# Differential attention in the second block of a two-block transformer kernel: scores kept in PSUM under a 64x64 corner mask, one square root for all heads, the first branch product placed ahead of the second branch's turns

## The reference, cut to what matters

```python
def differential_attention(q, k, v, lam, lam_init, subln_g):     # 4 heads, 512 tokens, blocks of 128 rows
    key_chunk = jnp.arange(s) // 64
    def block(args):
        qa, qb, bi = args
        q_chunk = (bi * 128 + jnp.arange(128)) // 64
        mask = key_chunk[None, :] <= q_chunk[:, None]
        s1 = (qa @ k1) * scale;  s2 = (qb @ k2) * scale
        p1 = softmax(where(mask, s1, -1e30));  p2 = softmax(where(mask, s2, -1e30))
        return (p1 - lam * p2) @ v
    out = rms_norm(out, subln_g) * (1.0 - lam_init)               # over each head's 128 columns
...
g_a, g_b = split(sigmoid(g + b_gate))
merged = g_a * (o_a @ w_branch_a) + g_b * (o_b @ w_branch_b)      # o_a: chunked attention with a relative bias
x = layer_norm(ALPHA * x + merged @ w_out)
```

## Time and profile before

| what | value |
|---|---|
| median of 3 runs | 2563.78 us (2562.53 to 2566.39) |
| the profiled execution's own time | 2561.58 us |
| its span, first to last instruction | 2559.7 us |
| mean granted TensorE clock | 0.95 |
| PE busy | 2356.5 us, 92% of the span |
| DVE / ACT busy | 1691.4 / 1241.1 us |
| attention B, first mask addition to last probabilities | 1906.3 to 2002.7 us |
| from there to the first branch product | 2002.7 to 2017.2 us |
| first branch product | 2017.2 to 2040.9 us |

### The profile page before, as it was taken

The page is one execution under the profiler, slowest core; times in us unless marked ns, Lnnn a source line. Parts: engine busy times, 40 slices in busy tenths (PEclk is TensorE's granted clock), DMA queues, the critical chain, the costliest instruction groups (busy, mean ns, idle before and its releaser), DMA issues.

```text
span 2559.7 us, 29221 instructions
## 1 busy us (share of the span) xinstructions
PE 2356.5 (92%) x10384; PEld 1851.3 (72%) x10384; DVE 1691.4 (66%) x1740; ACT 1241.1 (48%) x1214; POOL 414.1 (16%) x296
## 2 busy tenths in 40 slices
PE   5989876999999999999999999679998898999995
PEld 3649554788888888888888888566765676878874
DVE  4535446889988998899988998443556536333423
ACT  1123213676777677767776777332337532322320
POOL 2030043112222222212221222020200011000001
PEclk9999976999999999999999999879989898999998
DMA  7010153899999999999999999712210133122210
GB/s 283 1 50 1 57 193 118 320 387 370 371 370 386 375 370 370 384 379 368 369 385 377 370 368 361 235 70 78 80 36 34 65 121 111 66 99 99 99 66 33
DMA packets 141554, 555.04 MB, mean 217 GB/s; under 512 B 11200, under 2 KB 12352, under 8 KB 124528
## 3 DMA queue, kind: packets, MB, share of 16 engines
q1 hardware_dynamic: 129968, 512.46, 52.5%
q0 software_dynamic: 10368, 37.49, 5.8%
q10 hardware_dynamic: 1152, 4.19, 0.4%
HBM read 525.80 MB, written 28.31 MB: 216 GB/s over the span
## 4 chain that ended last, share of the span: by engine, by line
PE 87%; DVE 7%; ACT 3%; POOL 1%; issue 1%; DMA 1%; SPq 0%; POOLq 0%; ACTq 0%; DVEq 0%
PE PS L361 83%; PE PS L646 1%; PE PS L640 1%; DVE act L1489 1%; ACT act L1400 1%; DVE act L1492 1%; POOL act L2063 1%; DVE st L1477 1%; DVE small L1939 1%; DVE act L1937 1%; PE PS L516 1%; ACT L1411 0%; PE PS L818 0%; DVE ring_parts L1851 0%; DMA act<-ln_emb_b 0%
## 5 line engine op out<-in xcount | busy, mean ns | idle before, releaser
L361 PE MATMUL PS<-act_parts 128*128 128x512 f32 (+1 forms) x3300 | 1058.9, 398 | 14.2 <-issue 7.5
L1768 DVE TENSOR_TENSOR low<-ring,act_parts 128x2048 fp32r<-128x2048 f32 x396 | 886.2, 2292 | 38.3 <-ACT act_parts L1270 38.3
L361 PEld LDWEIGHTS PS<-act_parts 128*128 128x128 f32 (+1 forms) x3300 | 617.8, 189 | 177.7 <-issue 42.3
L1270 ACT ACTIVATE act_parts<-ring 128x2048 fp32r<-128x2048 f32 x396 | 731.7, 1911 | 11.1 <-PE PS L361 10.8
L361 PE MATMUL PS<-low,act_parts 128*128 128x512 f32 x1584 | 619.7, 391 | 0.0
L361 PE MATMUL PS<-act_parts,ring_parts 128*128 128x512 f32 x1216 | 380.8, 403 | 6.6 <-DVE act_parts L1991 3.7
L361 PEld LDWEIGHTS PS<-low,act_parts 128*128 128x128 f32 x1584 | 299.3, 189 | 58.3
L1851 DVE TENSOR_TENSOR ring_parts<-ring,ring_parts 128x4096 fp32r<-128x4096 f32 x30 | 132.7, 4423 | 231.8 <-ACT ring_parts L1339 231.7
L361 PEld LDWEIGHTS PS<-act_parts,ring_parts 128*128 128x128 f32 x1216 | 234.9, 193 | 70.1 <-issue 12.1
L361 PE MATMUL PS<-ring_parts,act_parts 128*128 128x512 f32 x1088 | 264.8, 397 | 12.3 <-DVE act_parts L2007 6.7
L361 PEld LDWEIGHTS PS<-ring_parts,act_parts 128*128 128x128 f32 x1088 | 207.3, 191 | 60.0 <-DVE act_parts L2007 7.1
(11 more groups left out here) (220 smaller groups left out, 1878.5 us busy)
## 6 DMA issues: line engine op xcount, KB each, us to landing
ring<-w_gate_up SPq DMA_DIRECT2D x264, 1024.0 KB, 8.0
ring<-w_down SPq DMA_DIRECT2D x132, 1024.0 KB, 7.4
ring<-w_ff SPq DMA_DIRECT2D x16, 2048.0 KB, 7.7
ring<-w_in SPq DMA_DIRECT2D x12, 2048.0 KB, 8.8
ring<-w_o SPq DMA_DIRECT2D x1, 4096.0 KB, 23.0
ring<-w_out SPq DMA_DIRECT2D x2, 2048.0 KB, 7.6
acc_d<-act SPq DMA_DIRECT2D x5, 512.0 KB, 2.6
act<-x SPq DMA_DIRECT2D x4, 512.0 KB, 4.9
```

The source lines that it names most:

```text
L361: return eng.matmul(o, lhsT, rhs, start=first, stop=last, **kw)
L1270: A_(W1hi[c % CS], W1[c], ACT.Copy).then_inc(sem["high"], 1)
L1768: tt(W1lo[c], W1[c], W1hi[c % CS].bitcast(F32), ALU.subtract).then_inc(sem["low"], 1)
```

## The change

1. Masking. `masked` waits for both score products, writes -1e30 with one memset into the 64x64 corner of both PSUM banks, and takes both maxima with one reduction over the two banks. The additions, the mask tile and POOL's two memsets are gone; POOL's signal is now `angles_done`. `scores_b` begins at an even bank, so that the two banks are neighbours. The exponentials read PSUM and write SBUF, and now the score banks come free with `expb`, not with the mask addition.
2. Normalisation. `square_b` leaves the sum of squares in one of 16 columns and copies the raw output to SBUF, which frees the bank (`ob_raw`). `out_b` is gone. After the loop ACT takes one square root of 16 columns, DVE one reciprocal, and `scale_heads` multiplies four 128x512 tiles by it. The gain `subg` is a column of one element per partition now and is applied in the high and low parts of the second half (`heads_high(1)`, `heads_low(1)`).
3. Order. Half A of the outputs is turned in iteration u = 16 of the loop, and the first branch product waits for its four low parts alone. Half B is turned after the fourth of the eight blocks of that product. On DVE the split of chunk 9 stands after the fourth of the branch multiplications, behind the low parts of half B; before, it stood ahead of all eight. On ACT the square root stands ahead of the sigmoids, and `heads_high(1)` behind them. `o2hi` and `o2lo` have a place of their own for each half.

A helper `affine` is added and not called. Core of the diff:

```diff
             def scores_b(u):
+                cur[0] += cur[0] % 2
...
-                    free[b] = past("sb_masked", 2 * u + m + 1)
+                    free[b] = past("expb", 2 * u + 2)
...
+            def turn_heads(g):
+                for t in range(NT):
+                    eng.wait_ge(*(past("ob_out", t + 1) if g else past("oa_out", UA)))
+                    b = next_bank(8 if g else 6)
+                    eng.wait_ge(*free[b])
+                    free[b] = past("o2T_lo", NT * g + t + 1)
+                    for j in range(4):
+                        ins = eng.transpose(PS[:, b, j * P:(j + 1) * P], XN[:, t, (4 * g + j) * P:(4 * g + j + 1) * P],
+                                            ident)
+                    ins.then_inc(put("o2T_psum", b), 1)
...
+                if u == UB:
+                    turn_heads(0)
...
-                eng.wait_ge(*past("o2T_lo", 2 * NT))
+                eng.wait_ge(*past("o2T_lo", NT * (br_ + 1)))
...
+                    if br_ == 0 and f == 3:
+                        turn_heads(1)
...
             def probs_b(u):
                 eng.wait_ge(*past("maxb", u + 1))
+                eng.wait_ge(*(past("pTb_psum", u - 1) if u >= 2 else past("pTa_psum", UA)))
                 for m, e in enumerate((e1b, e2b)):
-                    A_(e[:, u % 2, 0:n], e[:, u % 2, 0:n], ACT.Exp, scale=DH ** -0.5,
+                    b = bank_of("sb_psum", 2 * u + m + 1)
+                    A_(e[:, u % 2, 0:n], b[:, 0:n], ACT.Exp, scale=DH ** -0.5,
...
-                A_(hank[:, 0:P], b[:, 0:P], ACT.Square, accum_out=small[:, 24 + u % 2:25 + u % 2]).then_inc(
+                A_(hank[:, 0:P], b[:, 0:P], ACT.Square, accum_out=small[:, 48 + 4 * t + h:49 + 4 * t + h]).then_inc(
                     signal("act_step"), 1)
                 eng.wait_ge(*latest("act_step"))
-                A_(small[:, 26 + u % 2:27 + u % 2], small[:, 24 + u % 2:25 + u % 2], ACT.Sqrt,
-                          scale=1.0 / P, bias=EPS_2).then_inc(signal("ob_std"), 1)
+                A_(XN[:, t, 512 + h * P:512 + (h + 1) * P], b[:, 0:P], ACT.Copy).then_inc(signal("ob_raw"), 1)
...
+            A_(small[:, 48:64], small[:, 48:64], ACT.Sqrt, scale=1.0 / P, bias=EPS_2).then_inc(signal("ob_std"), 1)
             for f in range(KD):
                 A_(G2[:, f, :], G2[:, f, :], ACT.Sigmoid, bias=bgc[:, f:f + 1]).then_inc(signal("gate0_out"), 1)
+            heads_high(1)
             split_weights(9)
...
             def masked(u):
-                for m, e in enumerate((e1b, e2b)):
-                    tt(e[:, u % 2, 0:n], b[:, 0:n], maskb[:, S - n:S], ALU.add).then_inc(signal("sb_masked"), 1)
-                    eng.tensor_reduce(small[:, 32 + m:33 + m], e[:, u % 2, 0:n], AX.X, ALU.max).then_inc(
+                eng.wait_ge(*past("sb_psum", 2 * u + 2))
+                eng.memset(PS[0:DH, b - 1:b + 1, n - DH:n], NEG).then_inc(signal("sb_masked"), 1)
+                eng.tensor_reduce(small[:, 32:34], PS[:, b - 1:b + 1, 0:n], AX.X, ALU.max).then_inc(
...
+            scale_heads()
             for br_ in range(2):
-                split_weights((9, 11)[br_])
...
+                    if br_ == 0 and f == 3:
+                        heads_low(1)
+                        split_weights(9)
```

More of the change, by code:

```diff
@@ L1339, in split_weights, with high @@
                 A_(W2hi[n % NH], W2[n % NW], ACT.Copy).then_inc(signal("w_high"), 1)
-            def high(tag, XT):
-                for n in range(2 * NT):
+            def high(tag, XT, tiles=range(NT)):
+                for n in range(2 * tiles[0], 2 * tiles[-1] + 2):
                     t, hf = n // 2, n % 2
@@ L1419, in _ @@
                     square_b(u - 2)
+                if u == UB:
+                    heads_high(0)
                 if u < UB and u % 2:
@@ L1424, in _ @@
                         split_weights(8)
-            for n in range(2 * NT):
-                t, g = n // 2, n % 2
-                eng.wait_ge(*past("o2T_psum", n + 1))
-                A_(o2hi[:, 4 * g:4 * g + 4, o2_rows(t, g)], four(bank_of("o2T_psum", n + 1)),
-                   ACT.Copy).then_inc(signal("o2T_hi"), 1)
+            A_(small[:, 48:64], small[:, 48:64], ACT.Sqrt, scale=1.0 / P, bias=EPS_2).then_inc(signal("ob_std"), 1)
             eng.wait_ge(*past("bgc_in", 16))
@@ L1851, in split_weights, with low @@
                 tt(W2lo[n % NW], W2[n % NW], W2hi[n % NH].bitcast(F32), ALU.subtract).then_inc(signal("w_low"), 1)
-            def low(tag, XT, hi):
-                for n in range(2 * NT):
+            def low(tag, XT, hi, tiles=range(NT)):
+                for n in range(2 * tiles[0], 2 * tiles[-1] + 2):
                     t, hf = n // 2, n % 2
@@ L1983, in _ @@
                     split_weights(8)
-                if u >= 2:
-                    out_b(u - 2)
-            for n in range(2 * NT):
-                t, g = n // 2, n % 2
-                rows = o2_rows(t, g)
-                eng.wait_ge(*past("o2T_hi", n + 1))
-                tt(o2lo[:, 4 * g:4 * g + 4, rows], four(bank_of("o2T_psum", n + 1)),
-                   o2hi[:, 4 * g:4 * g + 4, rows].bitcast(F32), ALU.subtract).then_inc(signal("o2T_lo"), 1)
+                if u == UB:
+                    heads_low(0)
+            scale_heads()
             for br_ in range(2):
-                split_weights((9, 11)[br_])
                 if br_:
+                    split_weights(11)
                     split_weights(12)
```

101 lines of the change are left out of this document (56 added, 45 removed).

## The result

| | before | after |
|---|---|---|
| median of the runs, us | 2563.16 (2562.53 to 2566.39) | 2531.88 (2530.14 to 2534.67) |
| ratio, 95% interval | | 0.9879 [0.9863, 0.9894] |
| profiled execution, us | 2561.58 | 2530.14 |
| span, us; mean granted clock | 2559.7; 0.950 | 2528.3; 0.954 |

What follows compares the result with a forecast made beforehand. Attention B's chain of waits bounds the kernel, and PE its loop after the change. Loop, tail and branch 0 terms end branch 0 27.8 us earlier; 28 taken: 2561.58 to 2533.6, plus 2.2 gives 2535.8 us, range 2527 to 2545.

Steps and rivals of the forecast that it cites:

- The bound before: Attention B: a chain of mask, maximum, exponentials, mixing, copy, next mask, 23.05 us a head, with PE hardly in it.
- The loop, DVE: Attention B loop: fewer mask additions and no per-unit scaling cut the chain from 23.05 to 17.1 us a head.
- The loop, ACT: Attention B loop: 27 table loads, 34.6 us, leave ACT, few on the chain; exponentials from PSUM cost no more.
- The loop, PE: Attention B loop: PE needs 18.5 us a head against the chain's 17.1, becomes the bound; last `beside` ends at 1979.1.
- The loss to PE: Attention B loop: with PE as the bound, only 4.5 of DVE's 6 us a head count.
- The tail: Between last `beside` and branch 0: a new 2 us PE pause; branch 0 starts at 1987.2 instead of 2017.21.
- Branch 0: First branch product: 23.7 us plus 1.9 for half B's turns and 0.3 wait for chunk 9's split; ends at 2013.1.
- Contention in PSUM: Rival, loop: each exponential takes 0.3 us more, the chain grows to 19.5 a head; gain 20, time 2544; chance 0.14.
- The clock at full speed throughout: Rival, PE from the loop to branch 0: no long pause or slow beginning; gain 35, time 2529; chance 0.13.
- Order gives back part: Rival, branch 0: chunk 9's split comes late, 7 us lost before gate 1; gain 21, time 2543; chance 0.07.
- A load kept in the loop: Rival, ACT in the loop: compiler keeps a table load at each copy or square; no difference; chance 0.01.
- TensorE at 1.2 GHz throughout: Rival, loop: PE's 64.8 us take as long again, 37 us slower net, time 2600; chance 0.02.

Runs made afterwards that it cites:

- mask_and_order: Kernel after with the old normalisation put back (square root, reciprocal and scaling per unit, 27 table loads in the loop); 2545.6 us.
- after_best2: Kernel after with the splits of chunks 7 and 8 in quarters inside the loop and half A's high parts earlier; 2521.5 us, ratio 0.9836.
- norm_only: Kernel before with only the change's normalisation (one square root, scaling and gain after the loop), old masking and order; 2554.8 us.

## Why the prediction was right, and what in it was not

**The bound before** was read rightly: the chain from mask to mask. Every edit that shortened it shortened the kernel. But the way the chain takes was misread. It goes "mask, maximum, exponentials, mixing, copy, next mask" only in some units; in nine it goes through the root's table load, as here between units 12 and 13 and between 14 and 15 of the kernel before (chain of waits, start us, us, what):

```profile
1982.99 1.28 ACT L1411
...
1994.42 1.28 ACT L1411
```

**The loop, DVE.** The chain per head came out at 17.00 for 17.1, and that is luck in part. From the mask of unit 11 to that of unit 15 it takes 23.05 us before, 19.74 with the mask alone and 20.31 with the norm alone. So the masks gave 3.31 a head where 3.85 were booked, and the norm part 2.74 where 2.1 were; the two errors cancel. Successive operations of DVE overlap a little, so that from mask to scaled maxima the four units of a head shrank by 3.6 us and not 3.85; of these, with the mask alone, 0.2 are lost in unit 12, where the second table load ends behind the maxima. The prices of single operations that the sum took from the first block and from the additions held to 0.02 us.

**The loop, ACT.** "Few of them are on the chain" is the reading that failed. Of the loads, the 13 ahead of the exponentials did run beside DVE's masks, all but the one behind chunk 8's split. The other 14, ahead of the root, run beside mixing and copy, and the chain of waits passes through nine of them whole. What this was worth is another matter: mixing and copy end 0.4 us before the root at most, so the loads held DVE up for 1.6 us in five waits, 0.6 a head, and unit 8 for another 1.7 (mask_and_order against the kernel after). The prediction named these waits ("where DVE waited for the square root") and then put them at nothing. They are the greater part of the norm part's error; the 7.9 us booked for DVE's shorter queue (2.1 a head) were 7.4.

The Trainium skill, "ScalarE: Activation LUTs", section "Table sets: the hidden batching unit", says to do all exponentials together and then all square roots. That is what this part does, and the runs agree that it pays: putting 27 loads of 1.283 us and 16 roots back costs 9.4 us, for 34.6 us of loads on ACT. The 1.38 us of drain that the same page adds to a load ("What ACT_TABLE_LOAD costs") is not seen after the change either. ACT in order of time:

```profile
1985.41 1.28 ACT L1441 ACT_TABLE_LOAD   x1
1986.70 0.31 ACT L1441 ACTIVATE small<-small,colc 128x16 f32<-128x16 f32 x1
```

The root starts 0.01 us behind its load's end.

**The loop, PE.** "PE becomes the bound" was half right. PE takes 18.09 us a head (18.5 said) against the chain's 17.00. But the chain is held up at the split of chunk 8: from unit 8's mask to unit 9's it takes 1949.30 - 1939.63 = 9.67 us, 6.3 more than the 3.38 between the same two block sizes a head later. That eats its lead of 1.1 us a head, and the two arrive together: 69.9 us from first to last exponential, and PE at 1976.99. I had put 2.0 us of the split into PE's account, and a pause of 2.14 is there. The last `beside` ended at 1976.98 instead of 1979.1, and two terms are smaller than said. The slow beginning has a granted clock of 0.71 over 5.8 us, which is 1.7 of lost time and not 3.1. PE's steps were 18.09 / 4 = 4.52 a unit and not 4.63, 1.5 us over 14. With them, the measured first transposes and the measured pause the sum reads 1908.9 + 63.3 + 1.7 + 2.1 = 1976.0, 1 us short.

**The loss to PE** ("of DVE's 6 us a head only 4.5 count") did not show. The parts alone and the whole agree to 1 us. The old kernel's chain had the same split in it, and each part was cheaper or dearer than its term in the sum. A head's 6.05 us (23.05 - 17.00) are the 3.31 and 2.74 of the parts alone; what PE took back are the 0.73 us in which DVE waited for it.

**The tail.** 8.1 us from the last `beside` to branch 0 were said, 7.95 were measured, with the new wait of 2 us in its place. As a part of the change the order gained 7.8 to 8.8 us and gave 1.1 to 1.2 back.

**Branch 0.** 23.7 + 1.9 + 0.3 were said, 2011.29 - 1984.93 = 26.4 to the last gate multiplication were measured. But the four last of these run together behind chunk 9's split, so that their end says little. Gate 1's first weight load waits 0.2 us. The cover for chunk 9's split was as thin as the sum said, and it held. (The sum's terms for that split give 12.7 us and not the 12.9 written there, against PE's 12.8.)

**The rivals.** Contention in PSUM: refuted, 0.691 us for the longest exponential and 1.224 for a maximum over two banks. The clock at full speed throughout: not in the kernel after (0.71 at the beginning, 0.95 in the loop); nearly so in after_best2, without the split in front (0.98). Order gives back part: 1.2 us and not 7. A load kept in the loop: there is none between the first and the last exponential. TensorE at 1.2 GHz throughout: nowhere. Of the 3.3 us by which the change did better than said, the earlier end of the loop holds 2.1 and the tail 0.2; the last 1.0 is behind the start of branch 0.

## What to carry to other kernels

- Work of two engines that runs side by side covers each other. The table loads and DVE's scaling were worth 10.0 us of chain together, and the loads put back alone cost 8.1 of it. So price such work together, and don't read one's share from the run that puts it back alone: look in the trace for who waits.
- Where a chain and a full engine run level, the stage behind starts from the chain's last result. A lag that costs nothing in the loop is paid at its end, so follow the last exponential and not the last matmul.
- A long single operation (a weight split, 3.5 us on ACT and 4.4 on DVE) in the middle of a chain, or just ahead of it, can stand in its way in full. Two such splits in quarters, placed where the engine waits anyway, with half A's high parts sooner, brought 10 us, a third of what the whole change did; 8.1 of these came from the split ahead of the loop.

## What the runs showed of the hardware

- Reading PSUM cost neither engine anything: exponentials of 512 columns took 0.683 us in the mean from PSUM, 0.714 from SBUF; a maximum over 1024 columns of two banks 1.224 us, by the slope of the earlier trace rows 1.23.
- Writing to the strided place took nearly twice as long on both engines. ACT's high parts of 128x512 took 0.610 us in the median for half A and 1.140 for half B, DVE's low parts 0.68 and 1.164. Half B also has a per-partition scale, so the two are not told apart here; the earlier trace rows has the same pair of times without a scale, which speaks for the stride.
- The granted clock was 0.71 over 5.8 us behind a PE pause of 2.28 us. In after_best2, with a pause of 1.67 us ahead of it and none in the loop, it was 0.98 over the loop, with 0.50 in its first 1.4 us.
- Profiled executions scatter by up to 7 us through what happened far upstream of an edit, in norm_only between 300 and 600 us. Which edits come with a late start, and why, stays open.
